# One stage for input projection, GLA, rotary embedding, row turning and prompt compression

## The chip, the cores and the metric

One core of one Trainium2 chip runs the whole program. The metric is device microseconds for one execution. The core has five engines, each with its own instruction stream: TensorE (PE, matmuls; PEld is its weight load), VectorE (DVE), ScalarE (ACT), GpSimd (POOL) and SyncE (SP), which here only issues transfers. The streams are ordered among each other by semaphores alone.

## What is computed

One step of a decoder layer for 256 prompt tokens and 8 sequences of 8 new tokens, 320 columns in all, with 2048 features:

```python
x = layer_norm(ALPHA * x + 0.5 * swiglu(x, w_ffn1_in, w_ffn1_out), ln_g[0], ln_b[0])
m, ... = token_mixing(x, ...)
x = layer_norm(ALPHA * x + m, ln_g[1], ln_b[1])
x = layer_norm(ALPHA * x + 0.5 * swiglu(x, w_ffn2_in, w_ffn2_out), ln_g[2], ln_b[2])
...
# token_mixing
(gq, gk, gv, ga, gr, nq, kc, vc, ks, vs, kw, vw, ng) = jnp.split(h @ w_in, SPLIT_POINTS, axis=-1)
log_a = jax.nn.log_sigmoid((ga @ w_gla_gate2 + b_gla_gate2)) / GLA_TAU
o_g, gla_s = gla_chunked(gq, gk, gv, log_a, gla_s0)          # 4 heads, dk 128, dv 256
o_g = head_rms_norm(o_g, gla_norm_g) * jax.nn.silu(gr)
q = rope(nq, qpos); k rows of three branches = rope(kc | ks | kw, qpos)
k_cmp, v_cmp = compress(...)                                  # then sparse attention over three branches
return concat([o_g, o_n]) @ w_out, cmp_rows, slc_rows, win_all[:, -w_buf:], gla_s
```

## The kernel before

The program is a row of stages, each a block that ends with a barrier of all engines: first ffn, LayerNorm 0 with `projection`, two blocks of `gla`, `attention`, `mix_projection` with LayerNorm 1, second ffn, LayerNorm 2. Data lie feature-major: 128 features by 320 columns.

**Projection.** 44 output tiles of 128 features, in loops of 22 pairs. A unit is one tile: 16 k-tiles with three matmuls each (lines 292 to 294), since weights and activations are split into a high and a low part. SP loads 1 MB of a unit's weights (line 316) into one of two buffers, VectorE makes the high part (308) and the low part (310), TensorE multiplies, ScalarE evicts the bank (781). The columns for the gates (80 wide) are multiplied at the end, in fp32 (770). LayerNorm 0 also keeps ALPHA times x for the residual sum.

**First block of `gla`.** Logits of the decay gates (889), swap of halves for the rotary embedding (894; sine product on VectorE, 971, cosine product on GpSimd, 926, sum on VectorE, 975), turning of rows (`turns`, 909 and 904), prompt compression (917), the scan of the decays. SP issues the small loads, then one copy of the window cache from DRAM to DRAM (`out_win_s`, 861, 3968 KB), then the stores of turned rows.

**Second block of `gla`.** Nine levels of a tree of decays, all four heads at once. For each level VectorE makes a difference (1023 to 1037), ScalarE its exponential, GpSimd scales the keys (`k_level`, 1145) and VectorE the queries (1079), TensorE multiplies (scores, 1187 and 1182), VectorE merges the result by a mask (1049, 1051). Behind the levels stand, for the 64 new tokens, the products with the old state (1195, moving 8 columns each) and the outer products for the new state (1202). Then the outputs (1228 to 1234), the prompt's new state (1239) and the mean squares (1248). A record of an fp32 matmul stands twice in the trace; "x16" at 1195 is eight instructions.

Of the kernel before, what the change touches and what calls it, by code (L numbers as in the profile page):

```python
# [27 lines left out]
ACT = mybir.ActivationFunctionType  # L28
# [6 lines left out]
P = 128  # L35
# [93 lines left out]

def build(nc, A, O):  # L130
    ctx = ExitStack()
    with ctx:
# [6 lines left out]
        def sb(name, shape, dt=F32, scope=None):  # L139
            return (scope or ctx).enter_context(nc.sbuf_tensor(name, shape, dt))  # L140

        L.sem, L.sb = sem, sb
        L.bank = [ctx.enter_context(nc.psum_tensor(f"bank{i}", [P, 512], F32)) for i in range(8)]
        L.cst = sb("cst", [P, K_ALL])
        L.lvl = sb("lvl", [P, LEVELS, T], U8)
        L.ln_gb = sb("ln_gb", [P, 2, 3, KD])
        L.xT = sb("xT", [P, KD, T])
        L.raw = [sb(f"raw{a}", [P, KD * P]) for a in range(2)]
        L.proj = sb("proj", [P, NT, T])
        L.gate = sb("gate", [P, T])  # L150
        L.hid = [sb(f"cmp_hid{n}", [P, NB + 1, KV, NC]) for n in range(2)]
        L.cmp_bias = sb("cmp_bias", [P, 2])
        L.table = sb("table", [1, NB * NPG], I32)
# [23 lines left out]
        open_operands(L, "before")  # L177
        blocks = SampleBlocks(L)
        ffn(L, "ffn1", "w_ffn1_in", "w_ffn1_out", LoadInputs(L), side=blocks)
        projection(L, LayerNorm(L, 0), blocks)  # L180
        L.operands.close()
        with ExitStack() as mixing:
            L.kv_tok = sb("kv_tok", [P, 3, 12 * P], scope=mixing)
            L.gate_tok = sb("gate_tok", [P, 3, 48], scope=mixing)
            L.cmp_w2 = sb("cmp_w2", [P, 2, HD], scope=mixing)
            with ExitStack() as s:
                L.v_gla = sb("v_gla", [P, 3, GH * DV], scope=s)
                gla(L, s)
            with ExitStack() as s:
                attention(L, s)  # L190
        open_operands(L, "after")
        mix_projection(L)
        ffn(L, "ffn2", "w_ffn2_in", "w_ffn2_out", LayerNorm(L, 1))
        L.operands.close()
# [3 lines left out]
def open_operands(L, when):  # L198

    L.operands = ExitStack()  # L200
    L.xh = L.sb("xh_" + when, [P, KD, T], F32R, L.operands)
    L.xl = L.sb("xl_" + when, [P, KD, T], F32R, L.operands)
    L.wh = [L.sb(f"wh{a}_{when}", [P, KD * P], F32R, L.operands) for a in range(2)]
    L.wl = [L.sb(f"wl{a}_{when}", [P, KD * P], F32R, L.operands) for a in range(2)]
# [237 lines left out]
def ffn(L, name, w_in, w_out, before, side=None):  # L442
# [7 lines left out]
    scope = ExitStack()  # L450
    with scope:
        hh = L.sb(name + "_hh", [P, FC, T], F32R, scope)
        hl = L.sb(name + "_hl", [P, FC, T], F32R, scope)

        gate, up, hid = (L.proj[:, i] for i in range(3))
        part = [L.proj[:, 3 + a] for a in range(2)]
        product, hi_done = L.sem(name + "_product"), L.sem(name + "_hidden_hi")
        with nc.Block() as block:
            @block.sync
            def _(sp):  # L460
                def load_in(c, f):
                    for a in range(2):
                        load_unit(L, sp, f + (c * per + q0), a,
                                  wi[:, :, bass.ds(f * P + (c * (FC * P) + a * D_FF), P)], KD)

                before.sync(sp)
                load_in(0, 0)
                for c in range(CH):
                    if side:
                        side.sync(sp, 2 * c)  # L470
                    with sp.Fori(0 if c else 1, FC) as f:
                        load_in(c, f)
                    if side:
                        side.sync(sp, 2 * c + 1)
                    with sp.Fori(0, KD // 2) as n:
                        for a in range(2):
                            load_unit(L, sp, n + (c * per + (FC + q0)), a,
                                      wo[:, c * FC:(c + 1) * FC, bass.ds(n * (2 * P) + a * P, P)], FC)

            @block.vector  # L480
            def _(dve):
                before.vector(dve, lambda a: split_unit(L, dve, q0, a, L.loaded, 16, own0, KD))
                for c in range(CH):
                    with dve.Fori(0 if c else 1, FC) as f:
                        split_pair(L, dve, f + (c * per + q0), L.loaded, 16, f + (c * per + own0), KD)
                    with dve.Fori(0, KD // 2) as n:
                        split_pair(L, dve, n + (c * per + (FC + q0)), L.loaded, 16,
                                   n + (c * per + (FC + own0)), FC)

            @block.tensor  # L490
            def _(pe):
                before.tensor(pe)
                for a in range(2):
                    multiply_unit(L, pe, q0, a, KD, (L.xh, L.xl), before.ready if a == 0 else None)
                for c in range(CH):
                    def hidden_there(pe, k):

                        if k == 0:
                            pe.wait_ge(L.hidden_made, c * FC + (FC + h0))
                        if k == FC - 1:  # L500
                            pe.wait_ge(L.hidden_made, c * FC + (FC + h0 + 1))

                    with pe.Fori(0 if c else 1, FC) as f:
                        for a in range(2):
                            multiply_unit(L, pe, f + (c * per + q0), a, KD, (L.xh, L.xl))
                    if side:
                        side.tensor(pe, 2 * c)
                    with pe.Fori(0, KD // 2) as n:
                        for a in range(2):
                            multiply_unit(L, pe, n + (c * per + (FC + q0)), a, FC, (hh, hl),  # L510
                                          hidden_there if a == 0 else None)
                    if side:
                        side.tensor(pe, 2 * c + 1)

            @block.scalar
            def _(act):
                before.scalar(act)
                for c in range(CH):
                    with act.Fori(0, FC) as f:
                        act.wait_ge(L.multiplied[0], f + (c * per + (q0 + 2)))  # L520
                        act.wait_ge(L.hidden_made, f + (c * FC + (h0 + 1)))
                        act.activation(gate, L.bank[0][:, 0:T], ACT.Silu).then_inc(L.taken[0], 1)
                        act.wait_ge(L.multiplied[1], f + (c * per + (q0 + 2)))
                        act.activation(up, L.bank[1][:, 0:T], ACT.Copy).then_inc(L.taken[1], 1)  # L524
                    if side:
                        side.scalar(act, 2 * c)
                    with act.Fori(0, KD // 2) as n:
                        take_parts(L, act, part, n + (c * per + (FC + q0)), n + (c * (KD // 2) + y0), 0.5)
# [1240 lines left out]
```

## Time and profile before

| | us |
|---|---|
| median of 3 runs | 2886.5 |
| lowest, highest | 2880.16, 2900.79 |
| profiled execution, its own time | 2884.81 |
| its span in the trace | 2883.0 |
| TensorE busy in it | 2764.4 |
| VectorE, GpSimd, ScalarE busy | 1577.5, 790.2, 480.5 |

The span runs from the first to the last instruction that the profiler saw; the execution's own time has 1.8 us more. PEclk in a row is the clock granted to TensorE as a share of full speed: 1.00 is 2.4 GHz and 0.50 is 1.2 GHz.

### The profile page before, as it was taken

The page shows a single profiled execution, that of the slowest core. Times are in us where ns is not written, and L with a number is a line of the kernel's source. Part 1 is how long each engine was busy: PE and PEld are TensorE (multiplying, and loading weights), DVE is VectorE, ACT ScalarE, POOL GpSimd, SP SyncE. Part 2 cuts the span into 40 slices and gives each one's busy share as a digit, 9 for nine tenths or more (in the row PEclk, how much of TensorE's full clock was granted, in tenths as well). Part 3 has the DMA queues.
Part 4 walks back from the last instruction along what each step waited for, and adds up shares of the span by engine and source line. Part 5 has one row for each costly group of instructions (what it writes and reads, how often), then busy time and mean ns, then how long its engine had stood idle before and what let it go on. Part 6 is the DMA issues. An engine that isn't in the chain of part 4 may idle for free. (4 is left out here: it accounts for less than half of the span.)

```text
span 2883.0 us, 45361 instructions
## 1 busy us (share of the span) xinstructions
PE 2764.4 (96%) x17699; PEld 2638.6 (92%) x17699; DVE 1577.5 (55%) x1539; ACT 480.5 (17%) x1108; POOL 790.2 (27%) x580
## 2 busy tenths in 40 slices
PE   6999999999999999999898998979999999999997
PEld 5999999899999979998686777969999999999996
DVE  4555556455555564552747544565565565555555
ACT  2111001111100130001524541041100000000002
POOL 1331332232133520000424002543223322322353
PEclk9999999999999999999656887979999999999998
DMA  6555555455555445663321114435455455555542
GB/s 180 151 158 156 145 147 141 135 152 158 155 147 143 127 109 154 149 147 93 124 88 32 59 38 117 116 103 152 136 163 145 138 153 160 141 140 164 152 130 82
DMA packets 734086, 380.71 MB, mean 132 GB/s; under 512 B 65402, under 2 KB 729722, under 8 KB 733386
## 3 DMA queue, kind: packets, MB, share of 16 engines
q1 hardware_dynamic: 733754, 378.60, 48.1%
q10 hardware_dynamic: 272, 1.36, 0.1%
q8 instruction: 32, 0.52, 0.1%
q14 instruction: 28, 0.23, 0.0%
HBM read 370.60 MB, written 13.38 MB: 133 GB/s over the span
## 5 line engine op out<-in xcount | busy, mean ns | idle before, releaser
L292 PE MATMUL bank<-xh_before,wh_before 128*128 128x320 f32 x2112 | 659.4, 312 | 15.6 <-DVE wl_before L310 13.9
L293 PE MATMUL bank<-xl_before,wh_before 128*128 128x320 f32 x2112 | 656.8, 311 | 0.0
L294 PE MATMUL bank<-xh_before,wl_before 128*128 128x320 f32 x2112 | 656.6, 311 | 0.0
L292 PE MATMUL bank<-xh_after,wh_after 128*128 128x320 f32 x1664 | 521.1, 313 | 22.1 <-DVE wl_after L310 13.6
L308 DVE CAST wh_before<-raw 128x2048 fp32r<-128x2048 f32 (+1 forms) x196 | 219.8, 1121 | 574.4 <-PE bank L294 544.2
L293 PE MATMUL bank<-xl_after,wh_after 128*128 128x320 f32 x1664 | 518.0, 311 | 0.0
L294 PE MATMUL bank<-xh_after,wl_after 128*128 128x320 f32 x1664 | 517.8, 311 | 0.0
L310 DVE TENSOR_TENSOR wl_before<-raw,wh_before 128x2048 fp32r<-128x2048 f32 (+1 forms) x196 | 463.0, 2362 | 6.7
L308 DVE CAST wh_after<-raw 128x2048 fp32r<-128x2048 f32 (+1 forms) x168 | 184.9, 1101 | 435.2 <-PE bank L294 434.5
L292 PEld LDWEIGHTS bank<-xh_before,wh_before 128*128 128x128 f32 x2112 | 400.1, 189 | 19.3 <-issue 8.0
L310 DVE TENSOR_TENSOR wl_after<-raw,wh_after 128x2048 fp32r<-128x2048 f32 (+1 forms) x168 | 409.1, 2435 | 5.8
L293 PEld LDWEIGHTS bank<-xl_before,wh_before 128*128 128x128 f32 x2112 | 400.3, 190 | 0.5 <-issue 0.5
L294 PEld LDWEIGHTS bank<-xh_before,wl_before 128*128 128x128 f32 x2112 | 400.2, 189 | 0.0
L539 POOL TENSOR_TENSOR proj<-proj 128x320 f32<-128x320 f32 x88 | 125.1, 1421 | 886.2 <-ACT proj L524 886.2
L292 PEld LDWEIGHTS bank<-xh_after,wh_after 128*128 128x128 f32 x1664 | 315.1, 189 | 28.1 <-DVE wl_after L310 14.4
L293 PEld LDWEIGHTS bank<-xl_after,wh_after 128*128 128x128 f32 x1664 | 316.0, 190 | 0.0
L294 PEld LDWEIGHTS bank<-xh_after,wl_after 128*128 128x128 f32 x1664 | 315.7, 190 | 0.0
L292 PE MATMUL bank<-ffn_hh,wh_after 128*128 128x320 f32 x704 | 217.9, 310 | 0.9 <-POOL ffn_hl L544 0.9
L292 PE MATMUL bank<-ffn_hh,wh_before 128*128 128x320 f32 x704 | 217.9, 309 | 0.0
L293 PE MATMUL bank<-ffn_hl,wh_after 128*128 128x320 f32 x704 | 217.6, 309 | 0.0
L294 PE MATMUL bank<-ffn_hh,wl_before 128*128 128x320 f32 x704 | 217.5, 309 | 0.0
L293 PE MATMUL bank<-ffn_hl,wh_before 128*128 128x320 f32 x704 | 217.5, 309 | 0.0
(232 smaller groups left out, 3383.0 us busy)
## 6 DMA issues: line engine op xcount, KB each, us to landing
raw<-in_w_ffn_in SPq DMA_DIRECT2D x176, 1024.0 KB, 5.8
raw<-in_w_ffn_out SPq DMA_DIRECT2D x128, 704.0 KB, 4.9
raw<-in_w_in SPq DMA_DIRECT2D x36, 1024.0 KB, 5.7
raw<-in_w_in SPq DMA_DIRECT2D x16, 512.0 KB, 5.1
raw<-in_w_out SPq DMA_DIRECT2D x16, 512.0 KB, 4.4
raw<-in_w_out SPq DMA_DIRECT2D x64, 128.0 KB, 4.0
proj<-in_cache_cmp_kv SPq DMA_DIRECT2D x64, 64.0 KB, 2.5
raw<-in_state_gla SPq DMA_DIRECT2D x8, 512.0 KB, 4.6
```

The source lines that it names most:

```text
L292: pe.matmul(out, L.wh[a][:, w], hi[:, k], start=(k == 0), stop=False)
L293: pe.matmul(out, L.wh[a][:, w], lo[:, k], start=False, stop=False)
L294: last = pe.matmul(out, L.wl[a][:, w], hi[:, k], start=False, stop=(k == nk - 1))
L308: dve.tensor_copy(L.wh[a][:, 0:n], L.raw[a][:, 0:n]).then_inc(L.hi[a], 1)
L310: dve.tensor_tensor(L.wl[a][:, 0:n], L.raw[a][:, 0:n], L.wh[a][:, 0:n].bitcast(F32), ALU.subtract).then_inc(L.split[a], 1)
L539: pool.tensor_tensor(hid, gate, up, ALU.mult).then_inc(product, 1)
```

## The change

`projection` and both blocks of `gla` become one block, `front`, without loops: every instruction is written out. Units come in a new order (`UNITS`: GLA keys and queries, rows of keys and values, queries of the sparse attention, GLA values, GLA gates). Weights are loaded and split in halves of a unit (512 KB): four raw buffers, three for the high part, the low part written over the raw one. After a unit, TensorE does the pieces that the tables name for it: `spare_jobs` (gates, turns, rotary swap, compression, mean squares, prompt state), the scores of two heads of one level behind units 8 to 25, outputs of one head behind units 32, 34, 37 and 39 with the products with the old state now inside, and outer products behind these units and the next ones. The differences of the levels and the sum of the rotary embedding go from VectorE to GpSimd, the keys of one sequence (`k_one`) from ScalarE to GpSimd. The matmul for the gates is split in three like the units (48 matmuls instead of 16 in fp32). State of the GLA is loaded and stored by head (1 MB). The gates' Silu is done by ScalarE when it evicts the unit. LayerNorm 0 no longer keeps ALPHA times x: `attention` adds the high and low part again on GpSimd (`x_again`), before turned keys take the place of the low part, and `mix_projection` and LayerNorm 1 scale for it.

```diff
-            if not self.last and k >= 2:
+            if self.keeps and k >= 2:
...
-def projection(L, before, blocks):
...
+UNITS = [T_GK + i for i in range(4)] + [T_GQ + i for i in range(4)] + [T_KV + i for i in range(12)] + \
+        [T_NQ + i for i in range(8)] + [T_GV + i for i in range(8)] + [T_GR + i for i in range(8)]
...
+NSTEP = 2 * (LEVELS + 1)
...
+OUT_AT = {32: 0, 34: 1, 37: 2, 39: 3}
+OUTER_AT = {at + half: (h, half) for at, h in OUT_AT.items() for half in range(2)}
...
+            def load_half(j):
+                u, k = j // 2, slice(j % 2 * KH, j % 2 * KH + KH)
+                tile = UNITS[u]
+                if j >= 4:
+                    sp.wait_ge(w_used, j - 3)
...
+                c = columns(tile)
+                sp.dma_start(raw[j % 4][:].rearrange("p (k n) -> p k n", n=P), w_rows[:, k, c:c + P]
+                             ).then_inc(w_in[j % 4], 16)
...
+            for u in range(NU):
+                for j in (2 * u + 4, 2 * u + 5):
+                    if j < 2 * NU:
+                        load_half(j)
+                if u == 2:
+                    sp.wait_ge(blocks.hidden, 2)
+                    load_w1(0)
+                if u == 4:
+                    sp.dma_start(O["win_s"][0, :, 0:PAST - TS].rearrange("b r s k d -> b r (s k d)"),
+                                 A["cache_win_kv"][0, :, TS:PAST].rearrange("b r s k d -> b r (s k d)")
+                                 ).then_inc(L.stored, 16)
+                if u - 2 in KV_AT:
+                    freed(sp, ("kv_turn", KV_AT[u - 2]))
...
+                for after, h in OUT_AT.items():
+                    if u == after + 3:
+                        store_state(h)
+                        if h + 2 < GH:
+                            load_state(h + 2)
...
+            def split(j):
+                dve.wait_ge(w_in[j % 4], landed[j])
+                if j >= 3:
+                    dve.wait_ge(w_used, j - 2)
+                dve.tensor_copy(whi[j % 3][:], raw[j % 4][:]).then_inc(w_hi, 1)
+                dve.wait_ge(w_hi, j + 1)
+                dve.tensor_tensor(wlo[j % 4][:], raw[j % 4][:], whi[j % 3][:].bitcast(F32), ALU.subtract
+                                  ).then_inc(w_lo, 1)
...
+            for u in range(NU + 1):
+                if 2 * u + 3 < 2 * NU:
+                    split(2 * u + 3)
...
+                if u - AT_LEVELS - 1 in range(NSTEP):
+                    merge(u - AT_LEVELS - 1)
+                if u - 1 in ROPE_AT:
+                    by_sine(ROPE_AT[u - 1])
+                if u - 1 in OUTER_AT:
+                    state(*OUTER_AT[u - 1])
...
+                if 2 * u + 4 < 2 * NU:
+                    split(2 * u + 4)
...
+                if s in range(2, NSTEP):
+                    q_level(s)
...
+            for u in range(NU + 2):
...
+                if s in range(NSTEP):
+                    k_level(s)
+                if s + 2 in range(NSTEP):
+                    difference(s + 2)
+                if u - 2 in ROPE_AT:
+                    rope(ROPE_AT[u - 2])
+                if u - 1 in ROPE_AT:
+                    by_cosine(ROPE_AT[u - 1])
...
+                for half in range(2):
+                    j = 2 * u + half
+                    pe.wait_ge(w_lo, j + 1)
...
+                        pe.matmul(out, whi[j % 3][:, c], L.xh[:, k], start=(k == 0), stop=False)
+                        pe.matmul(out, whi[j % 3][:, c], L.xl[:, k], start=False, stop=False)
+                        mm = pe.matmul(out, wlo[j % 4][:, c], L.xh[:, k], start=False, stop=(k == KD - 1))
+                    mm.then_inc(w_used, 1)
...
+                    for q in range(NB):
+                        mm = pe.matmul(b[:, TP + q * TS:TP + (q + 1) * TS], st[h % 2][:, q, c * P:(c + 1) * P],
+                                       QS[:, h, q * TS:(q + 1) * TS], start=False, stop=(q == NB - 1),
+                                       skip_group_check=True)
...
+            for u in range(NU):
+                unit(u)
+                for job in spare_jobs(u):
+                    make_spare(job)
...
+                if u - AT_LEVELS in range(NSTEP):
+                    scores(u - AT_LEVELS)
+                if u in OUT_AT:
+                    outputs(OUT_AT[u])
+                if u in OUTER_AT:
+                    outer(*OUTER_AT[u])
...
+            for k in range(KD):
+                pool.tensor_tensor(x_again[:, k], x_high[:, k].bitcast(F32), x_low[:, k].bitcast(F32), ALU.add
+                                   ).then_inc(rebuilt, 1)
...
+                take_parts(L, act, part, n + q0, n + y0, 1.0 / ALPHA)
```

SyncE's queue around the window copy, before: `cmp_w` are the compression's weights, `kv_tok` the turned rows.

```order
L858 DMA raw<-in_cmp_w 128x16x128
L857 DMA cmp_w<-in_cmp_w 128x64
L858 DMA raw<-in_cmp_w 128x16x128
L861 DMA out_win_s<-in_cache_win_kv 8x8x15872
L871 DMA out_cmp_p<-kv_tok 128x512 [waits turned_out]
```

The copy stands behind all loads of its block. After, about unit 4, with `half_raw` the buffers of half a unit's weights:

```order
L898 DMA proj<-in_cmp_w 128x16x128 [waits blocks_hidden]
L894 DMA half_raw_2767<-in_w_in 128x8x128 [waits half_used]
L894 DMA half_raw_2768<-in_w_in 128x8x128 [waits half_used]
L894 DMA half_raw_2765<-in_w_in 128x8x128 [waits half_used]
L894 DMA half_raw_2766<-in_w_in 128x8x128 [waits half_used]
L945 DMA out_win_s<-in_cache_win_kv 8x8x15872
L894 DMA half_raw_2767<-in_w_in 128x8x128 [waits half_used]
L894 DMA half_raw_2768<-in_w_in 128x8x128 [waits half_used]
```

The copy now has loads of weights ahead of it and behind it in one queue.

TensorE at one level of the second GLA block, before: `gla_sq` and `q_level`, `k_level` are scaled queries and keys, `q_samples` times `raw` is the product with the old state.

```order
L1187 MATMUL bank<-gla_sq 128x128 [waits gla_lv_merged]
L1187 MATMUL bank<-gla_sq 128x128
L1187 MATMUL bank<-gla_sq 64x64
L1195 MATMUL bank<-q_samples,raw 128x8 [waits state_in0,gla_o_k_tok]
L1195 MATMUL bank<-q_samples,raw 128x8 x7
L1202 MATMUL bank<-v_gla,k_one 128x256 [waits gla_s_k]
L1202 MATMUL bank<-v_gla,k_one 128x256 x3
L1187 MATMUL bank<-q_level,k_level 128x128 [waits gla_lv_merged,gla_lv_k,gla_lv_q]
L1187 MATMUL bank<-q_level,k_level 128x128
L1187 MATMUL bank<-q_level,k_level 64x64
```

The four heads of a level stood together, then state and outer products. After, the end of a unit behind which a rotary swap (1338), a turn (1345) and scores of two heads (1392) stand:

```order
L1303 MATMUL bank<-xh_before,half_lo_2772 128x320
L1338 MATMUL bank<-proj,cst 128x320 [waits half_taken,spare_free0]
L1345 MATMUL bank<-cst,proj 128x128 [waits half_taken,front_roped,spare_free1]
L1345 MATMUL bank<-cst,proj 128x128 x3
L1392 MATMUL bank<-q_level_2788,k_level_2790 128x128 [waits front_merged,front_q,front_k]
L1392 MATMUL bank<-q_level_2788,k_level_2790 128x128 x3
L1301 MATMUL bank<-xh_before,half_hi_2773 128x320 [waits half_lo,half_taken]
```

Between the last matmul of one unit and the first of the next there are now pieces, each with waits of its own. After, on TensorE too, the end of the outputs of one head, with the old state's products (1413) inside and outer products (1423) behind:

```order
L1410 MATMUL bank<-gla_att,v_samples 128x64
L1413 MATMUL bank<-q_samples,state_2802 128x8 x8
L1406 MATMUL bank<-gla_att,proj 128x128
L1407 MATMUL bank<-gla_attx,proj 128x128
L1408 MATMUL bank<-gla_att,proj 128x128
L1410 MATMUL bank<-gla_att,v_samples 128x64
L1413 MATMUL bank<-q_samples,state_2802 128x8 x8
L1423 MATMUL bank<-v_samples,k_one_2804 128x256 [waits front_k_one]
L1423 MATMUL bank<-v_samples,k_one_2804 128x256 x3
L1301 MATMUL bank<-xh_before,half_hi_2773 128x320 [waits half_lo,half_taken]
```

The products with the old state moved from the levels into the outputs, and a unit (1301) follows.

## Rows read from the trace of the kernel before

**Rows 1.** The page's first part: busy time, share and instructions of each engine.

```profile
PE 2764.4 (96%) x17699; PEld 2638.6 (92%) x17699; DVE 1577.5 (55%) x1539; ACT 480.5 (17%) x1108; POOL 790.2 (27%) x580
```

**Rows 2.** Windows by stage: PE, PEld, DVE, ACT, POOL busy, PEclk, DMA share, GB/s.

```profile
1035.00:1355.00 320.00, 316.59 (x2104) 312.41 (x2103) 155.71 (x95) 26.32 (x58) 5.49 (x6) 0.98 0.55 134
1355.00:1410.00 55.00, 40.86 (x193) 27.24 (x191) 27.68 (x40) 27.77 (x39) 20.91 (x30) 0.80 0.49 166
1410.00:1525.00 115.00, 110.71 (x453) 92.71 (x453) 60.12 (x115) 35.65 (x43) 36.67 (x17) 0.59 0.22 70
1525.00:1760.00 235.00, 206.07 (x1159) 159.73 (x1158) 130.82 (x484) 113.08 (x437) 32.48 (x37) 0.72 0.16 46
```

**Rows 3.** Timeline of TensorE behind the projection: start, time, line, count, idle.

```profile
1349.87 8.78 PE L770 MATMUL bank<-xT,w_small 128*80 128x320 f32 x32
...
1364.28 4.63 PE L889 MATMUL bank<-gate,gw 16*128 16x320 f32 x8 [5.63 <-DMA norm_g<-in_gla_norm_g]
...
1386.62 6.75 PE L909 MATMUL bank<-cst,proj 128*128 128x128 f32 x60
...
1394.35 7.39 PE L917 MATMUL bank<-q_level,raw 128*128 128x60 f32 x64
...
1528.02 1.17 PE L1443 MATMUL bank<-cmp_hid,cmp_w 128*64 128x270 f32 x4 [2.53 <-PEq L1015]
```

**Rows 4.** Timeline of ScalarE: the evictions of units 2 and 43.

```profile
1061.54 0.44 ACT L781 ACTIVATE proj<-bank 128x320 f32 x1 [6.60 <-PE bank L294]
...
1350.17 0.44 ACT L781 ACTIVATE proj<-bank 128x320 f32 x1 [6.60 <-PE bank L294]
```

**Rows 5.** TensorE at the projection's start: timeline, and a window (PEclk behind busy).

```profile
1044.61 0.64 PE L292 MATMUL bank<-xh_before,wh_before 128*128 128x320 f32 x1 [2.30 <-DVE wl_before L310]
...
1049.00:1050.00 1.00, 1.00 (x5) 0.50 1.06 250
```

**Rows 6.** Second GLA block on TensorE: timeline, and a window.

```profile
1463.22 1.85 PE L1195 MATMUL bank<-q_samples,raw 128*128 128x8 f32 x16
1465.00 2.37 PE L1202 MATMUL bank<-v_gla,k_one 64*128 64x256 f32 x8
...
1474.84 3.78 PE L1187 MATMUL bank<-q_level,k_level 128*128 128x128 f32 x16
...
1512.55 0.49 PE L1228 MATMUL bank<-gla_att,v_gla 128*128 128x128 f32 x2
...
1517.45 3.72 PE L1239 MATMUL bank<-v_gla,k_tok 128*128 128x256 f32 x16
1521.01 4.47 PE L1248 MATMUL bank<-gla_sq,cst 128*128 128x320 f32 x16
...
1467.00:1468.00 1.00, 1.00 (x4) 0.50 0.00 0
```

**Rows 7.** Transfers: SP's issue, a window, the program's first 36 us, whole program.

```profile
1366.12 3.36 SPq L861 DMA_DIRECT2D out_win_s<-in_cache_win_kv  x1
...
1385.00:1390.00 5.00, 4.52 (x35) 3.78 (x34) 4.90 (x8) 2.74 (x6) 3.83 (x7) 1.00 0.47 203
...
raw<-in_w_ffn_in SPq DMA_DIRECT2D x2, 1024.0 KB, 19.6
...
raw<-in_w_ffn_in SPq DMA_DIRECT2D x176, 1024.0 KB, 5.8
```

**Rows 8.** VectorE by line, 1030 to 1412 us; GpSimd by line, 1355 to 1530 us.

```profile
L310 DVE TENSOR_TENSOR wl_before<-raw,wh_before 128x2048 fp32r<-128x2048 f32 x43 | 98.6, 2293 | 1.5
L308 DVE CAST wh_before<-raw 128x2048 fp32r<-128x2048 f32 x43 | 52.8, 1228 | 145.8 <-PE bank L294 145.8
...
L1145 POOL TENSOR_TENSOR k_level<-proj,decay_e 128x1280 f32<-128x1280 f32 x5 | 14.6, 2929 | 38.5 <-ACT decay_e L1112 28.6 <-PE bank L1187 9.9
L926 POOL TENSOR_TENSOR decay_e<-proj,cst 128x320 f32<-128x320 f32 x14 | 12.0, 863 | 335.2 <-POOLq L721 320.6 <-DVE proj L975 14.6
L1147 POOL TENSOR_SCALAR proj<-proj,norm_g 128x320 f32<-128x320 f32 x8 | 9.3, 1170 | 0.0
```

More of the change, by code:

```diff
@@ L175, in build, with operands @@
         L.h = 0
-        open_operands(L, "before")
+        operands(L, "before", M_XH, M_XL)
         blocks = SampleBlocks(L)
         ffn(L, "ffn1", "w_ffn1_in", "w_ffn1_out", LoadInputs(L), side=blocks)
[L180 to L191, printed above, removed]
+        L.kv_tok = at("kv_tok", M_KVT, [P, 3, 12 * P])
+        L.gate_tok = at("gate_tok", M_GT, [P, 3, 48])
+        front(L, LayerNorm(L, 0), blocks)
+        attention(L)
+        operands(L, "after", M_X0, M_XL)
         mix_projection(L)
-        ffn(L, "ffn2", "w_ffn2_in", "w_ffn2_out", LayerNorm(L, 1))
-        L.operands.close()
+        ffn(L, "ffn2", "w_ffn2_in", "w_ffn2_out", LayerNorm(L, 1, EPS / ALPHA ** 2))
         write_outputs(L, LayerNorm(L, 2))
[L198 to L204, printed above, removed]
+def operands(L, when, hi, lo):
+    L.xh = L.at("xh_" + when, hi, [P, KD, T], F32R)
+    L.xl = L.at("xl_" + when, lo, [P, KD, T], F32R)
+    L.wh = [L.at(f"wh{a}_{when}", M_W + (2 + a) * 8192, [P, KD * P], F32R) for a in range(2)]
+    L.wl = [L.at(f"wl{a}_{when}", M_W + (4 + a) * 8192, [P, KD * P], F32R) for a in range(2)]
 class LoadInputs:
@@ L796 @@
+        if self.keeps:
+            pool.wait_ge(self.L.ln["kept"], KD)
 class Chain:
@@ L1253, in attention @@
-def attention(L, s):
+                        mm = pe.transpose(b[0:rows, t * P:(t + 1) * P], proj[:, T_GV + i, t * P:t * P + rows], ident)
+                if job[0] == "ms":
+                    h = job[1]
+                    pe.wait_ge(squared, h + 1)
+                    for c in range(2):
+                        mm = pe.matmul(b[:, 0:T], L.cst[:, K_RMS:K_RMS + P], sq[:, c], start=(c == 0), stop=(c == 1))
+                if job[0] == "s_prompt":
+                    for i in range(2):
+                        h = 2 * job[1] + i
+                        for t in range(2):
+                            mm = pe.matmul(b[:, i * DV:(i + 1) * DV], k_tok[:, t, h * P:(h + 1) * P],
+                                           v_gla[:, t, h * DV:(h + 1) * DV], start=(t == 0), stop=(t == 1))
@@ new lines, in outer @@
+            def outer(h, half):
+                pe.wait_ge(one_made, 2 * h + half + 1)
+                for i in range(4):
+                    if i % 2 == 0 and (h or half):
+                        pe.wait_ge(st_made, 4 * (2 * h + half) - 2 + i)
+                    mm = pe.matmul(bank[4 + i // 2][:, i % 2 * DV:(i % 2 + 1) * DV], k_one[half][0:NS, i],
+                                   v_gla_s[0:NS, h * DV:(h + 1) * DV], start=True, stop=True)
+                    if i % 2:
+                        mm.then_inc(st_mult, 1)
@@ new lines, in _ @@
+            before.tensor(pe)
+            blocks.tensor_hidden(pe, 1)
+            for u in range(NU):
+                unit(u)
+                for job in spare_jobs(u):
+                    make_spare(job)
+                if u == AT_LOGITS:
+                    pe.wait_ge(small_in, 48)
+                    pe.wait_ge(gates_made, 1)
+                    for h in range(GH):
+                        pe.matmul(bank[2 + h][:, 0:T], gw2[64:80, h * P:(h + 1) * P], L.gate[64:80, :],
+                                  start=True, stop=True).then_inc(logit, 1)
+                if u - AT_LEVELS in range(NSTEP):
[4 more added lines that the diff above has]
+                    outer(*OUTER_AT[u])
```

1452 lines of the change are left out of this document (766 added, 686 removed).

## Prediction

> **What bounds the kernel now.** I read the page's first part, then windows by stage, then the timelines of the stretch that the change rewrites. TensorE is busy for 96% of the span [rows 1], so time can only come from making it idle less, from work that it does at the lower clock, or from less work. By stage [rows 2]: the projection is full (316.59 of 320 us busy, clock 0.98), units 2 to 43 follow each other at 288.63/41 = 7.04 us [rows 4], and VectorE is half idle there, ScalarE and GpSimd almost wholly. The first GLA block has TensorE busy for 41 of 55 us at 0.80. The second has it busy for 111 of 115 us, but at 0.59: a busy TensorE that is not at its peak. The stretch that goes is that from the gates' matmul at 1349.87 to the first matmul of attention at 1528.02, 178.15 us [rows 3]. What counts is how much of it is really work at full clock, since that must now stand between the units.
>
> **The pieces at full clock.** TensorE's work is in order, so each piece between two units lengthens the stage by its own time. By rows where the clock was 1.00:
> - Gates: now 48 matmuls of 320 columns. A unit's 48 take 7.04 [rows 4], so 7.0 (8.8 before [rows 3]).
> - Logits and rotary swap: 8 and 28 records of 320 columns in fp32; L770 gives 8.78/32 = 0.274, so 9.9.
> - Turns of rows: 6.75 for 60 [rows 3], and 18 more of keys and gates at the same 0.1125, 2.0.
> - Compression 7.4 [rows 3].
> - Scores: 168 records. Sixteen took 3.78 at half clock [rows 6], 0.118 each at full; larger groups nearer 0.13 as an estimate. I take 21.
> - Outputs: four groups from 1512.55 to 1517.45 [rows 6], 1.225 each, eight of them: 9.8.
> - Products with the old state: eight times 1.78 (from 1463.22 to 1465.00) [rows 6]: 14.2.
> - Outer products: eight times 2.37 at nearly full clock [rows 6]: 19.0, 15.1 if half of the 3.78 for the scores is the better guide.
> - Mean squares and prompt state: 4.3 and 3.6 [rows 6].
>
> Together 7.0 + 9.9 + 8.8 + 7.4 + 21 + 9.8 + 14.2 + 19.0 + 7.9 = 105 us, 100 to 108. Against 178.15 this alone is a gain of 73 us.
>
> **What comes on top.**
> - Start. TensorE waits 2.30 us for unit 1's low part and then runs at 0.50 until 1050 [rows 5], since one engine splits whole units: 1.23 + 2.29 us [rows 8]. With halves the first split after LayerNorm is half as long. I take -2.5, from -3 to 0.
> - Window copy. It ran at a DMA share of 0.47 and 203 GB/s [rows 7], so 3968 KB take some 20 us, after an issue of 3.36. Before, nothing that TensorE needed soon stood behind it. Now the loads of weights from half 14 on stand behind it in SP's queue, as the order shows. That a load behind others waits for them is seen at the program's start: the first two of the ffn's 1 MB loads took 19.6 us to land, the others 5.8 [rows 7]. When SP issues the copy, TensorE has done half 9 and has halves 10 to 13 ahead, 14.1 us with the gate turns 14.4. Half 14 lands after 20 to 23.4 us plus its own half of 5.8, and its split takes 1.8: 24.7 to 28.1. TensorE waits 10 to 14 us behind unit 6, and restarts at half clock, which by the 5.4 us of the start [rows 5] costs 2.7. I take +15. Low end 0, as the copy keeps only half of the DMA engines busy and loads might pass it; high end 20.
> - Clock at the outputs. After 1.85 us of products with 8 columns and the outer products behind them the clock was 0.50 at 1467 [rows 6]. The outputs of one head have two such runs, and outer products follow, before a unit. If the clock falls each time and comes back after some 5.4 us, four times up to 5.5 us are lost. I take half: +10, from 0 to 22.
> - Tail. The last eviction (0.44 [rows 4]), GpSimd's scaling of it by norm_g (1.17 [rows 8]) and the barrier with its start of the next block (2.53 [rows 3]) are not hidden any more; the root of the mean squares lies beside them. +3.5, from 2.5 to 6.
> - VectorE and GpSimd. A unit of units 8 to 25 needs on VectorE a split (3.5), two merges and a product of queries (at most 3.3: the second block's 60.12 us on VectorE [rows 2] over 18 steps of two heads, with differences and state in it), and a sine product (under 0.9): at most 7.7 of the 8.5 to 9.5 us of such a unit with its pieces. GpSimd needs keys of two heads (half of 2.93), a difference (not seen on GpSimd; between a product of keys, 1.46, and twice that), and two rotary operations (0.86 each) [rows 8]: 4.7 to 6.1. Both have room, so nearly all is hidden; +6 for waits of single pieces, 0 to 25.
> - `x_again` in attention: 16 sums of 0.86 [rows 8], 13.8 us on GpSimd at its start, where GpSimd is busy for 32 of 235 us [rows 2]; ahead only of the turned keys. +1, 0 to 5, which is what it costs if the keys come first.
> - LayerNorm 0 without its copies on ScalarE, stores of rows, loads of state by head, Silu in the eviction: nothing, hidden by TensorE's 7 us units, as ScalarE is busy for 26 of 320 us there [rows 2]. If the state came late, the outputs would wait; it is asked for at unit 28 and used at 32, four units or 30 us later.
>
> **Sum** against the profiled execution's 2884.81: -178.15 + 105 - 2.5 + 15 + 10 + 3.5 + 6 + 1 = -40.2, so 2845; I say 2846. The profiled execution is 1.7 us under the median of 2886.5, which is nothing here. All low ends together give 2805, all high ones 2893. About 1%, 29 us, is what a measurement of this kernel tells from no change.
>
> **Two rules beside the rows.** On the copy: the DMA share of 0.47 says that half of the engines moved it [rows 7]. The Trainium skill, "DMA: Bandwidth & Descriptors", section "Why a DMA increments its semaphore by 16 and not by 1", says that a transfer is spread over the largest number of engines, up to 16, that divides both outer dimensions; by that rule the outer dimension of 8 gives 8 of 16, and the trace agrees (0.47). The same page, "Queues, rings and completion order", has each engine take its descriptors in the order of the ring. By it the loads behind must wait on those 8 engines, which is the +15 and not the 0.
>
> On the pieces: 60 turns in a row began at 1386.62 [rows 3], and the window 1385 to 1390 has the clock at 1.00 [rows 7]. The Trainium skill, "TensorE: Matmul & The Clock Gate", section "Part 4: PE-mode transpose", says that transposes don't count as busy for the full clock. That rule speaks against the change: it would have the turns pull the units' clock down. The trace does not agree for these 6.75 us; what it would make of the time is the third rival.
>
> **Rivals.**
> 1. *The copy holds nothing up*, since its 0.47 leaves half of the DMA engines and the stage before needs only 134 GB/s [rows 2]. Then the 15 us are not lost: about 2830. For it: share and rate; against it: the 19.6 us of loads in a queue [rows 7].
> 2. *VectorE or GpSimd is late at each of units 8 to 25*, as a difference or a product on GpSimd takes longer beside VectorE (2.93 us for keys [rows 8] may already be that). A wait of 2 us at each of 18 units, with the clock unhurt, is +36: about 2881. Against it: the room in the count above.
> 3. *Slower: the pieces pull the clock down over the whole stretch.* Place: units 8 to 40, where pieces of 2 to 8 us stand between units. In attention short matmuls keep the clock at 0.72, in the second GLA block at 0.59 with TensorE busy nearly throughout [rows 2]. The stretch has 33 units and 95 us of pieces, 327 us of work; x of it at half clock adds 327 times x. It eats the gain of 40 from x = 0.12 on, and shows as slower by 1% from 0.21. At the 0.80 of the first GLA block [rows 2] over all of it the price is 327 times 0.25, 82, less the 10 that are counted: 2918. Against it: units of 7 us are dense and back at full clock after 5.4, and turns, compression, outputs and mean squares ran at 1.00 here.
>
> **How the numbers follow.** Forecast near 2846 (2830 to 2862): 0.53. Rival 1, 2830 and a little below: 0.14. Rival 2, 2865 to 2890: 0.19. Rival 3, above 2893: 0.09. The rest, 0.05, is a gain beyond 2812. Faster by over 1% means under 2857.6: most of the forecast (0.46) with rival 1, the rest and a little of rival 2, 0.66. Within 1%: 0.07 of the forecast, nearly all of rival 2 and a part of rival 3, 0.26. Slower: 0.08. The range goes from 2812 to 2888: below it lie the low ends together, above it rival 3 and the high ends together; 0.16 is left out. The forecast's own range is 2830 to 2862.
>
> **What would show it.** Right: unit to unit 7.04 us plus the pieces, PEclk at 1.00 from unit 8 to 31; one wait of 10 to 14 us on TensorE at unit 7 for the low part of half 14; PEclk below 1.00 behind units 32 to 40; the first matmul of attention some 40 us earlier than 1528. Rival 1: no wait at unit 7. Rival 2: short waits of TensorE for scores or low parts at each unit, with VectorE or GpSimd busy without a gap. Rival 3: PEclk near 0.7 in units 8 to 31. I would be wrong with a wait that I have counted as hidden (state, keys of one sequence, stores), or if the ffn stages, which the change leaves alone, move.

## The result, and the profile after

| | before | after |
|---|---|---|
| median, us | 2886.57 (4 runs) | 2855.05 (4 runs) |
| lowest, highest | 2880.16, 2900.79 | 2849.15, 2858.44 |
| profiled execution, its span | 2884.81, 2883.0 | 2854.97, 2853.1 |

The ratio is 0.9863, with a 95% interval from 0.9832 to 0.9894: a gain of 1.4%, clear of no change. The forecast was 2846, with a range from 2812 to 2888.

The page's first part, after: TensorE has 28 us less of busy time, GpSimd 71 us more; the shares of TensorE and VectorE are those of [rows 1].

```profile
PE 2736.4 (96%) x17715; PEld 2622.2 (92%) x17715; DVE 1578.3 (55%) x1595; ACT 474.0 (17%) x1116; POOL 861.7 (30%) x660
```

The windows by stage, after, with the columns of [rows 2]:

```profile
1035.00:1100.00 65.00, 61.80 (x370) 57.65 (x368) 34.55 (x42) 21.54 (x33) 10.61 (x13) 0.92 0.49 149
1100.00:1122.00 22.00, 9.35 (x50) 9.38 (x51) 7.49 (x8) 1.19 (x2) 2.74 (x2) 0.69 0.48 151
1122.00:1290.00 168.00, 167.62 (x1167) 161.91 (x1167) 114.99 (x149) 42.22 (x72) 82.64 (x77) 1.00 0.54 129
1290.00:1343.00 53.00, 53.00 (x362) 52.30 (x360) 30.82 (x35) 4.73 (x15) 10.57 (x11) 1.00 0.68 186
1343.00:1440.00 97.00, 97.00 (x533) 88.69 (x532) 34.17 (x50) 10.62 (x26) 9.42 (x9) 0.82 0.40 115
1440.00:1480.00 40.00, 40.00 (x240) 37.05 (x240) 18.62 (x27) 3.65 (x8) 4.46 (x3) 0.91 0.46 132
...
1490.59:1726.24 235.65, 205.26 (x1157) 158.70 (x1157) 134.82 (x480) 111.18 (x433) 45.61 (x53) 0.71 0.16 46
```

The last row is attention, from its first matmul to the first of the next stage. The same stretch before:

```profile
1528.02:1759.60 231.58, 205.18 (x1156) 159.30 (x1157) 129.13 (x480) 111.42 (x433) 32.43 (x37) 0.71 0.17 47
```

The reader is to see four things. Units 8 to 31, with their pieces between, have TensorE busy but for 0.4 us and the clock at 1.00 (1122 to 1343). Ahead of them TensorE was idle for 13 of 22 us. Behind them it is busy throughout at 0.82 and 0.91. And attention, which the change hardly touches, takes 4.1 us more at the same mean clock, 0.71.

TensorE's waits from 1000 to 1530, after (what waits, for whom; us in all, times, longest): one long wait, nothing for levels, state or stores, and 0.4 us for one turn (L1345). The other rows left out lie in LayerNorm 0 and in attention.

```profile
PE bank L1301 <- DVE half_lo L983: 14.0, 2, 13.3
...
PE bank L1301 <- DVE xl_before L702: 2.2, 5, 0.6
...
PE bank L1345 <- DVE rope_sin L1029: 0.4, 1, 0.4
```

ScalarE's evictions of units 1, 6 and 7, after. Unit 7 came 22.64 us behind unit 6, where a unit alone takes 7.04 [rows 4]: 15.6 us are the wait and its restart.

```profile
1053.55 0.44 ACT L1097 ACTIVATE proj<-bank 128x320 f32<-128x320 f32 x1 [9.81 <-PE bank L1303]
...
1099.39 0.44 ACT L1097 ACTIVATE proj<-bank 128x320 f32<-128x320 f32 x1 [5.14 <-PE bank L1303]
...
1122.03 0.44 ACT L1097 ACTIVATE proj<-bank 128x320 f32<-128x320 f32 x1 [20.81 <-PE bank L1303]
```

The last unit's eviction, and then TensorE's first matmul of attention, which stood at 1528.02 [rows 3] and comes 37.43 us earlier:

```profile
1488.64 0.44 ACT L1097 ACTIVATE proj<-bank 128x320 f32<-128x320 f32 x1 [2.22 <-PE bank L1303]
```

```profile
1490.59 0.68 PE L1645 MATMUL bank<-cmp_hid,cmp_w 128*64 128x270 f32 x4 [1.99 <-PEq L878]
```

**The ledger.** From unit 1's eviction at 1053.55 to unit 43's at 1488.64 are 435.09 us. Without 42 units of 7.04 us (295.7) and the 15.6 of unit 7, 123.8 are left for pieces and clock. The lost clock is read from windows of 4 us from 1340 to 1460: each has lost 4 times (1 less PEclk), 20.5 in all. So the pieces themselves took 103 us. The stretch removed begins 0.3 us ahead of unit 43's eviction (1349.87 and 1350.17), and so the tail is counted from 0.3 us ahead of the eviction at 1488.64.

| term, us | forecast | measured |
|---|---|---|
| stretch removed | -178.15 | -178.15 |
| pieces | +105 | +103 |
| start | -2.5 | -0.95, 0.4 of it from the stage ahead |
| window copy | +15 | +15.6 |
| clock at the outputs | +10 (0 to 22) | +20.5 |
| tail | +3.5 | +2.3 |
| waits of pieces | +6 (0 to 25) | +0.4 |
| attention | +1 (0 to 5) | +4.1 |
| everything behind | 0 | +3.4 |

The sum of what was measured is -29.8, against -29.9 between the two spans.

### The profile page after: what moved, and what is told of

Its sections match the earlier page's. It is cut to its first block and busy times, and to the rows that moved or that the text cites. A ratio compares the mean times of both kernels' runs of the same rounds, so it can differ in the third digit from the quotient of the medians.

```text
span 2853.1 us, 45328 instructions
## 1 busy us (share of the span) xinstructions
PE 2736.4 (96%) x17715; PEld 2622.2 (92%) x17715; DVE 1578.3 (55%) x1595; ACT 474.0 (17%) x1116; POOL 861.7 (30%) x660
## 5 line engine op out<-in xcount | busy, mean ns | idle before, releaser
L318 PE MATMUL bank<-xh_before,wh_before 128*128 128x320 f32 x1408 | 438.3, 311 | 11.4 <-DVE wl_before L336 11.4
L319 PE MATMUL bank<-xl_before,wh_before 128*128 128x320 f32 x1408 | 437.5, 311 | 0.0
L320 PE MATMUL bank<-xh_before,wl_before 128*128 128x320 f32 x1408 | 437.5, 311 | 0.0
L336 DVE TENSOR_TENSOR wl_before<-raw,wh_before 128x2048 fp32r<-128x2048 f32 (+1 forms) x152 | 362.8, 2387 | 5.2
L318 PEld LDWEIGHTS bank<-xh_before,wh_before 128*128 128x128 f32 x1408 | 266.6, 189 | 12.3 <-issue 7.6
L319 PEld LDWEIGHTS bank<-xl_before,wh_before 128*128 128x128 f32 x1408 | 266.6, 189 | 0.2 <-issue 0.2
L320 PEld LDWEIGHTS bank<-xh_before,wl_before 128*128 128x128 f32 x1408 | 266.5, 189 | 0.0
L1301 PE MATMUL bank<-xh_before,half_hi 128*128 128x320 f32 x704 | 230.2, 327 | 16.2 <-DVE half_lo L983 14.0
L1302 PE MATMUL bank<-xl_before,half_hi 128*128 128x320 f32 x704 | 223.5, 317 | 0.0
L1303 PE MATMUL bank<-xh_before,half_lo 128*128 128x320 f32 x704 | 223.2, 317 | 0.0
```

The costliest lines, as they stand in the source:

```text
L318: pe.matmul(out, L.wh[a][:, w], hi[:, k], start=(k == 0), stop=False)
L319: pe.matmul(out, L.wh[a][:, w], lo[:, k], start=False, stop=False)
L320: last = pe.matmul(out, L.wl[a][:, w], hi[:, k], start=False, stop=(k == nk - 1))
L336: dve.tensor_tensor(L.wl[a][:, 0:n], L.raw[a][:, 0:n], L.wh[a][:, 0:n].bitcast(F32), ALU.subtract).then_inc(L.split[a], 1)
L1301: pe.matmul(out, whi[j % 3][:, c], L.xh[:, k], start=(k == 0), stop=False)
L1302: pe.matmul(out, whi[j % 3][:, c], L.xl[:, k], start=False, stop=False)
```

## The experiments

Three questions were open: what made unit 7 wait, what made the clock fall behind units 32, 34, 37 and 39, and why attention grew. The place of a stage is read from TensorE's first matmul in it, since that does not hang on what happens behind it. It does hang on the start: unit 1's eviction, which none of the edits touches, stands at 1051.76 to 1054.26 in these kernels, for 1053.55 in the change, and this is said where it matters. Times are medians, ratios are to the kernel before on the same chip. Three kernels have one time only, and so no ratio. Of the five ratios only that of e7_both lies clear of the change's interval; for the others the places in the traces decide, each trace one execution.

**The window copy left out** (e1_no_copy)

```diff
-                if u == 4:
-                    sp.dma_start(O["win_s"][0, :, 0:PAST - TS].rearrange("b r s k d -> b r (s k d)"),
-                                 A["cache_win_kv"][0, :, TS:PAST].rearrange("b r s k d -> b r (s k d)")
-                                 ).then_inc(L.stored, 16)
...
```

> The copy of the window cache is left out (those rows of win_s stay unwritten), nothing else is changed. Theory: the one wait of 13.3 us on TensorE at unit 7, and the half clock behind it, come from loads of weights that stand behind the copy. Then the wait is gone, units 6 and 7 follow each other at some 7.0 us instead of 22.6, and the time is 15 to 16 us less, near 2839.5. Rival: unit 7 waits for something else that falls into the same place (the 1 MB load of the compression's weights two units earlier, or VectorE, which has the scan of the decays there). Then a wait of 10 us or more stays and the time stays within 4 us of 2855.

2841.69 us, ratio 0.9829 (0.9785 to 0.9874). The evictions of units 6 and 7 in this kernel stand 7.04 us apart, and attention begins at 1473.40, 17.2 us earlier than with the copy. Of these, 1.8 us lie ahead of unit 1's eviction (1051.76 for 1053.55), so 15.4 are the copy's:

```profile
1097.60 0.44 ACT L1093 ACTIVATE proj<-bank 128x320 f32<-128x320 f32 x1 [5.14 <-PE bank L1299]
...
1104.64 0.44 ACT L1093 ACTIVATE proj<-bank 128x320 f32<-128x320 f32 x1 [5.20 <-PE bank L1299]
```

The rival is out: the compression's weights and the scan are still there, and nothing waits. In the changed kernel itself SP's issue of the copy, and then VectorE's first work on half 14, show the mechanism:

```profile
1084.98 0.87 SPq L945 DMA_DIRECT2D out_win_s<-in_cache_win_kv  x1
```

```profile
1110.55 0.69 DVE L981 CAST half_hi<-half_raw 128x1024 fp32r<-128x1024 f32 x1 [18.55 <-DMA half_raw<-in_w_in]
```

VectorE waited 18.55 us for that one load of 512 KB, and TensorE, which had four halves in hand, waited 13.3 us for the low part that VectorE made of it.

**The copy in eight pieces** (e2_spread)

```diff
-                if u == 4:
...
+                if u - 4 in range(NB):
+                    sp.dma_start(O["win_s"][0, u - 4, 0:PAST - TS].rearrange("r s k d -> r (s k d)"),
+                                 A["cache_win_kv"][0, u - 4, TS:PAST].rearrange("r s k d -> r (s k d)")
+                                 ).then_inc(L.stored, 16)
...
```

> The copy is made in eight transfers of 496 KB, one behind the loads of each of units 4 to 11; all outputs are written. Theory (loads wait for what stands ahead in the queue): each transfer holds the next loads up by some 2.5 us, less than the three halves that are in hand (10.6 us), so TensorE does not wait: 15 us less than 2855, near 2840. Rival: any DRAM to DRAM copy beside the loads slows them by its share of the DMA engines, whole or in pieces, so that 13 us of waiting come back in pieces of 1 to 2 us: near 2853.

2840.29 us, ratio 0.9821 (0.9777 to 0.9864): as without a copy. TensorE's waits over the stage in this kernel have no entry of over 0.7 us for a low part:

```profile
PE bank L1301 <- DVE xl_before L702: 2.2, 5, 0.6
PE bank L1645 <- PEq L878: 2.0, 1, 2.0
PE bank L1301 <- DVE half_lo L983: 0.7, 1, 0.7
```

So the bytes of the copy cost nothing; its length in the queue did.

**The copy over 16 instead of 8** (e2b_sixteen)

```diff
-                    sp.dma_start(O["win_s"][0, :, 0:PAST - TS].rearrange("b r s k d -> b r (s k d)"),
-                                 A["cache_win_kv"][0, :, TS:PAST].rearrange("b r s k d -> b r (s k d)")
+                    sp.dma_start(O["win_s"][0, :, 0:PAST - TS].rearrange("b r s k d -> b (r s k d)").rearrange("b (c x) -> c b x", c=16),
+                                 A["cache_win_kv"][0, :, TS:PAST].rearrange("b r s k d -> b (r s k d)").rearrange("b (c x) -> c b x", c=16)
```

> The copy stays one transfer in its place, but its outer dimension is 16 instead of 8. Theory: half of the DMA engines moved it at 203 GB/s; with all of them it takes some 10 us instead of 20, so the wait at unit 7 falls from 13.3 to 3 to 5 us, and with a shorter stretch at half clock the time to some 2845. Rival: memory sets the rate of the copy, not the number of engines: window rows show the same 200 GB/s, the wait stays 12 to 14 us and the time 2855.

2853.77 us, ratio 0.9868 (0.9824 to 0.9913): by time no different from the change. The trace tells more: half 14 landed at 1102.65 instead of 1110.55, and the longest wait fell from 13.3 to 6.6 us. TensorE's wait for the low part, then VectorE's first work on half 14:

```profile
PE bank L1301 <- DVE half_lo L983: 7.3, 2, 6.6
```

```profile
1102.65 1.28 DVE L981 CAST half_hi<-half_raw 128x1024 fp32r<-128x1024 f32 x1 [11.36 <-DMA half_raw<-in_w_in]
```

Between theory (3 to 5) and rival (12 to 14), nearer to the theory: the wider copy held half 14 up for less long (VectorE's wait fell by 7.2 us, from 18.55 to 11.36), but not by the 10 us that the theory's rate would give. Attention began 6.1 us earlier in this trace (0.7 of them already at unit 1's eviction) and took 239.4 instead of 235.7; the medians differ by 1.3 us.

**Products with the old state among the unit's matmuls** (e5_state_in_unit)

```diff
...
+                        if u - 1 in OUT_AT:
+                            with_state(OUT_AT[u - 1], k)
...
-                    for q in range(NB):
-                        mm = pe.matmul(b[:, TP + q * TS:TP + (q + 1) * TS], st[h % 2][:, q, c * P:(c + 1) * P],
...
-MS_AT = {at + 1: h for at, h in OUT_AT.items()}
+MS_AT = {at + 2: h for at, h in OUT_AT.items()}
```

> The 16 products with the old state of a head are no longer done in a row inside the outputs: one stands behind each k-tile of the unit that follows. Mean squares move one unit later. Same instructions, all outputs written. Theory: the clock falls at each of the four outputs since products with 8 columns stand there in a row for 1.8 us twice; mixed among the unit's matmuls they leave the clock at 1.00, and the 20 us that the half clock costs in 1343 to 1456 are back: near 2835. Rival: the outer products (64 rows) and the length of the stretch between two units make the clock fall; then PEclk still falls to 0.50 behind units 32, 34, 37 and 39 and the time is 2850 to 2856.

2836.86 us, ratio 0.9806 (0.9756 to 0.9856). In the changed kernel the clock fell ahead of any outer product in all four heads: in the first 0.6 us behind the first row of these products, in the others inside the second row (near 1380.1, 1417.6 and 1448.3, by windows of 1 us). The timeline of the first head and its windows:

```profile
1343.55 1.95 PE L1413 MATMUL bank<-q_samples,state 128*128 128x8 f32 x16
...
1346.40 0.69 PE L1410 MATMUL bank<-gla_att,v_samples 64*128 64x64 f32 x2
1347.02 3.58 PE L1413 MATMUL bank<-q_samples,state 128*128 128x8 f32 x16
1350.53 2.07 PE L1423 MATMUL bank<-v_samples,k_one 64*128 64x256 f32 x4
```

```profile
1344.00:1345.00 1.00, 1.00 (x11) 1.00 1.03 305
1345.00:1346.00 1.00, 1.00 (x10) 0.97 0.57 164
1346.00:1347.00 1.00, 1.00 (x5) 0.50 0.00 0
```

The second row of the second head, and the window in which its clock fell:

```profile
1378.81 2.46 PE L1413 MATMUL bank<-q_samples,state 128*128 128x8 f32 x16
1381.20 3.78 PE L1423 MATMUL bank<-v_samples,k_one 64*128 64x256 f32 x8
```

```profile
1380.00:1381.00 1.00, 1.00 (x7) 0.54 0.00 0
```

With one product behind each k-tile, three of the four falls are gone; windows of this kernel (units with old state in the first three), and TensorE's timeline at the fourth:

```profile
1330.00:1370.00 40.00, 39.21 (x263) 1.00 0.47 132
1370.00:1410.00 40.00, 39.23 (x266) 1.00 0.55 159
1410.00:1450.00 40.00, 37.69 (x229) 0.91 0.46 132
```

```profile
1440.67 0.28 PE L1293 MATMUL bank<-q_samples,state 128*128 128x8 f32 x2
1442.11 3.19 PE L1429 MATMUL bank<-v_samples,k_one 64*128 64x256 f32 x8 [1.15 <-DVE state L1039]
```

The fourth fall, near 1442.7, came behind a wait of 1.15 us for VectorE's state, which this order makes new (3.9 us over four such waits), and 0.6 us into outer products. Attention began at 1475.05, 15.5 us earlier. Of these, 1.8 us lie ahead of unit 1's eviction (1051.79), so 13.8 are left of the 20.5 that the clock had cost.

**One of eight of these products** (e3_no_state)

```diff
-                    for q in range(NB):
+                    for q in (NB - 1,):
```

> Of the eight products with the old state in each half of a head's outputs only the last is done (the new tokens' outputs lack the others). Copy as in the change. Theory: these products in a row make the clock fall; with two left of sixteen the clock stays at 1.00 behind units 32, 34, 37 and 39, and the stage is shorter by 12.5 us of products and by some 20 us of half clock: attention begins near 1458 instead of 1490.6. Rival: the outer products or the plain length of work between units are the cause: the clock still falls to 0.50 four times and attention begins near 1478.

2824.29 us. Attention begins at 1457.25, 0.8 us from what the theory said, and the stretch of the four outputs has no fall in it:

```profile
1340.00:1455.00 115.00, 115.00 (x722) 1.00 0.52 149
```

**Outer products of 32 columns** (e4_small_outer)

```diff
-                    mm = pe.matmul(bank[4 + i // 2][:, i % 2 * DV:(i % 2 + 1) * DV], k_one[half][0:NS, i],
-                                   v_gla_s[0:NS, h * DV:(h + 1) * DV], start=True, stop=True)
+                    mm = pe.matmul(bank[4 + i // 2][:, i % 2 * DV:i % 2 * DV + 32], k_one[half][0:NS, i],
+                                   v_gla_s[0:NS, h * DV:h * DV + 32], start=True, stop=True)
```

> The outer products have 32 moving columns instead of 256 (the new state is not right); the products with the old state stay in a row. Theory: the clock still falls behind units 32, 34, 37 and 39, since it fell within the products with the old state before an outer product had begun; only the time of the outer products goes: some 15 us at full clock and up to 7 more where they ran at half, so attention begins between 1466 and 1476. Rival: outer products make it fall; then PEclk is 1.00 throughout and attention begins near 1455.

2837.47 us. The clock falls at all four outputs as before, the first time at the end of 1344 to 1346, with no outer product yet (it begins at 1349.04). Windows, then the timeline:

```profile
1344.00:1346.00 2.00, 2.00 (x16) 0.88 0.23 68
1346.00:1348.00 2.00, 2.00 (x11) 0.50 0.00 0
```

```profile
1345.52 3.58 PE L1413 MATMUL bank<-q_samples,state 128*128 128x8 f32 x16
1349.04 1.91 PE L1423 MATMUL bank<-v_samples,k_one 64*128 64x32 f32 x8
```

Attention begins at 1478.74, 11.9 us earlier and not the 15 at least that both stories of the size wanted: the outer products fell from 23.1 to 12.0 us of busy time and no further, since a matmul of 32 columns still took 0.27 us at full clock where one of 256 took 0.38. The cause of the falls stands: the products with 8 columns in a row.

**The sums of x later** (e6_late_sum)

```diff
-            for k in range(KD):
-                pool.tensor_tensor(x_again[:, k], x_high[:, k].bitcast(F32), x_low[:, k].bitcast(F32), ALU.add
-                                   ).then_inc(rebuilt, 1)
-
             ch = Chain(pool, o_step)
...
                 pool.tensor_tensor(proj[:, T_OG + n], proj[:, T_GV + n], proj[:, T_GR + n], ALU.mult)
+            for k in range(KD):
+                pool.tensor_tensor(x_again[:, k], x_high[:, k].bitcast(F32), x_low[:, k].bitcast(F32), ALU.add
+                                   ).then_inc(rebuilt, 1)
```

> The 16 sums that make x again stand behind GpSimd's other work of attention instead of ahead of it; all outputs are written. Attention, from its first matmul to the first of the next stage, took 231.6 us before the change and 235.7 after. Theory: the sums slow VectorE beside them (its steps of 0.28 us took 0.43 to 0.60 while they ran), so TensorE's long waits at 1503 to 1512 go (231.5 to 232.5 us), if VectorE is not just as critical 50 us later, where the sums then stand; if it is, 3 to 4 us come back there and the stage keeps its 235 us. Rival: the sums cost nothing and the four us come from elsewhere (the places of the buffers, the mean squares' root): waits at the start stay as they are, and so does the 235.

2845.46 us, attention 228.5 us. That number is not the effect: in the second half of attention the clock goes up and down differently in each kernel, and its length went from 228.5 (mean clock 0.74) to 241.7 (0.69) over the ten kernels. The first part can be compared, since from some 10 us on the clock is 0.50 there in each of them: from the first matmul to the first turned old keys it took 70.05 us before the change, 74.36 after it, 74.4 to 74.5 in the seven other kernels with the sums at the start, and 72.75 here. GpSimd's sums, after; then a step of VectorE beside them and the step at 1513.19; then the same two steps here, where no sums run beside them:

```profile
1497.58 13.20 POOL L1746 TENSOR_TENSOR x_again<-xh_before,xl_before 128x320 f32<-128x320 f32 x16
```

```profile
1505.07 0.89 DVE L1723 TENSOR_SCALAR probs<-probs,stat 128x128 f32<-128x128 f32 x1
...
1513.19 0.35 DVE L1688 TENSOR_TENSOR scores<-bank,cst 128x256 f32<-128x256 f32 x1
```

```profile
1502.75 0.28 DVE L1723 TENSOR_SCALAR probs<-probs,stat 128x128 f32<-128x128 f32 x1
...
1507.63 0.36 DVE L1688 TENSOR_TENSOR scores<-bank,cst 128x256 f32<-128x256 f32 x1
```

Counted from VectorE's first copy in attention, the second of these steps comes after 20.25 us in the change, after 15.88 here and after 15.90 in the kernel before. So the sums cost 4.4 us through VectorE, whose steps took 0.84 to 0.96 us beside them for 0.23 to 0.28. Later, at 1543.86 to 1556.95, they slowed the same steps again (L1723 764 and L1725 575 ns on average from 1535 to 1565, where the change has 533 and 455), and only 1.6 us were left at the first turned old keys. Neither the whole of the theory's 3 to 4 us nor the rival's nothing: most is given back.

**Copy, products and outer products together** (e7_both)

```diff
-OUTER_AT = {at + half: (h, half) for at, h in OUT_AT.items() for half in range(2)}
+OUTER_AT = {at + 1 + half: (h, half) for at, h in OUT_AT.items() for half in range(2)}
```

with the edits of e2_spread and e5_state_in_unit.

> The copy in eight pieces and the products with the old state among the unit's matmuls together, and the outer products one unit later, since one of them waited up to 1.2 us for VectorE and the clock then fell once. Theory: 15 us for the copy, 20 for the clock, 4 for these waits, less 2 of overlap: PEclk 1.00 from unit 2 to the end of the stage, attention begins near 1455, and the time is some 2818, a ratio of 0.974 to before. Rival: with the copy's waits gone the loads of state or the stores meet the loads of weights, and 5 to 10 us come back as waits for state at the outputs: 2824 to 2830.

2820.48 us (2814.91 to 2826.15, 6 runs), ratio 0.975 (0.9717 to 0.9782): faster than the change, whose interval lies wholly above this one. The whole stretch from unit 8 to the end of the stage in one window, then attention's first matmul:

```profile
1122.00:1455.00 333.00, 331.98 (x2245) 1.00 0.54 145
```

```profile
1456.75 0.68 PE L1651 MATMUL bank<-cmp_hid,cmp_w 128*64 128x270 f32 x4 [1.99 <-PEq L878]
```

1.00 throughout, and 33.8 us earlier than in the change, of the 36.1 that copy and clock had cost. The theory's place (near 1455) and time (some 2818) both came. Neither state nor stores make TensorE wait. Of this, 5.9 us went again in attention, which took 241.5 us here.

## Why the prediction was right

The forecast named the time within 0.3% and, of its two disputed places, got one exactly and one at its far end. A part of this closeness is luck: the gain of 40 us came to 30. Clock, behind attention, attention, start and copy cost 19 us more than was priced, and 9 us came back from waits, pieces and tail that cost less.

- **Pieces.** Durations at full clock from rows of the kernel before carried over: 105 said, 103 measured. It is the sum that this bears out, not each price: a group of outer products took 1.94 us at full clock in e5_state_in_unit and not 2.37, nearer to the prediction's other guide, and other pieces made up for it. That they do not add waits was the point on which the whole gain hung, and the trace has 0.4 us of them.
- **Window copy.** Right in place (unit 7), wait (13.3 in 10 to 14) and sum (15.6 for 15). e1 and e2 show it, e2b that the rate of the copy sets its size. The Trainium skill, "DMA: Bandwidth & Descriptors", section "Queues, rings and completion order", has descriptors taken in the order of the ring on each engine; the trace agrees, with a load of 512 KB that landed behind 3968 KB of copy although, by the share of 0.47 [rows 7], half of the engines had none of it.
- **Clock at the outputs.** Right in kind, mis-sized: the step "I take half: +10" came to 20.5, as the clock fell at each of the four outputs and not at every other. The rows of before showed a fall behind 1.85 us of such products and outer products [rows 6]; that there would be two such runs per head should have put the value near the high end. e3, e4, e5 and e7 show that the products with 8 columns do it, when they stand in a row.
- **Rival 3**, the clock pulled down over the whole stretch, did not come: 1.00 from 1122 to 1343, with 48 of the 60 turns, behind units 14 to 32, and all scores in it. The Trainium skill, "TensorE: Matmul & The Clock Gate", section "Part 4: PE-mode transpose", has the full clock not engage for transposes; the traces do not agree, at 1.00 after the change with these turns, and at 1.00 before it through 60 turns in a row of 6.75 us (1385 to 1395; [rows 3], [rows 7]).
- **Rival 2**, VectorE or GpSimd late at units 8 to 25, did not come: TensorE idled 0.4 of 168 us from 1122 to 1290, with VectorE busy for 115 and GpSimd for 83. The 6 us for it were too many.
- **Start.** -2.5 was mis-sized: the split of half a unit let unit 1 begin 0.65 us earlier (1043.96 for 1044.61), as unit 0 itself ended 1 us later behind LayerNorm, and the restart at half clock stayed. The tail cost 2.3 for 3.5.
- **Attention.** 4.1 us in place of 1, within the 0 to 5: the sums were costed as a wait for turned keys, and cost through VectorE instead, which slowed beside them (4.4 us, e6). That the whole stage shows so nearly the same is partly chance, as its clock differs between kernels.
- **Behind attention** 3.4 us were lost that the sum had not; they lie in pieces of 0.7 (mix projection), 1.1 (LayerNorm 1) and 1.7 us (second ffn and LayerNorm 2), and no experiment touches them. In e7_both the same instructions of the first two took 117.0 and 20.1 us, as before the change (117.3 and 20.1), so these are not shown to be a cost of it. They stay open; executions of one kernel differ by more.
- **Range.** The low ends add up to 2806, where the prediction has 2805; nothing hangs on it.

## What to carry to other kernels

Before work is put between the units of a full TensorE, price it at full clock, and look which pieces can't hold that clock: here long rows of matmuls with few columns, which left the clock alone once they were mixed in among wide ones. A transfer that nobody waits for belongs behind the loads that somebody does wait for, or in pieces shorter than what is in hand. And an engine that has time to spare may still slow its neighbour: read the neighbour's durations beside it, not its idle share.

## What was not expected of the hardware

- In one head the granted clock went from 1.00 to 0.50 just ahead of 1346, 0.6 us behind one row of 16 records with 8 columns, 1.81 us long; in the others it went inside the second such row. TensorE was busy throughout. The same 16 products, one behind each three matmuls of 320 columns, left it at 1.00 in all four heads of e7_both. With them mixed in, the clock fell once, in e5_state_in_unit, 0.6 us into outer products behind a wait of 1.15 us; which of the two did it is not shown, and in e7_both, which has neither the wait nor the fall, outer products stand between units too.
- Where the clock rises and falls in attention differs between kernels that are the same there, but for the place of the sums in one: 0.69 to 0.74 on average, and 13 us of its length.
- Beside sums of 128 by 320 on GpSimd, VectorE's steps of 128 by 128 took up to 960 ns for 280.
